# A decoder trunk with attention, gMLP and routed experts: side work of the gMLP dealt out anew over its steps, and weights loaded earlier

## What is computed

```python
for i in range(DEPTH):                       # DEPTH = 2
    h = x * (1 + sc_m) + sh_m
    y = sliding_window_sink_attention(h, ...) if i == 0 else chunked_spatial_gating(h, ...)
    x = layer_norm(DEEPNORM_ALPHA * x + (1 + gt_m) * y, ...)
    h = x * (1 + sc_f) + sh_f
    y = hierarchical_moe(h, ...)             # 4 groups of 8 experts, top 1 group, top 2 experts
    x = layer_norm(DEEPNORM_ALPHA * x + (1 + gt_f) * y, ...)

def chunked_spatial_gating(h, ...):          # the gMLP, chunks of 128 tokens
    u, v = split(gelu(h @ w_in + b_in))      # 2048 columns each
    v = layer_norm(v)
    mixed = einsum('gts,bnsgc->bntgc', tril(w_s), v) + b_s
    return (u * mixed) @ w_out + b_out
```

## Time and profile before

| | us |
|---|---|
| median of 3 runs | 2449.65 |
| the profiled execution: time, and its span | 2451.3, 2449.9 |
| TensorE busy, share of the span | 1326.5, 54% |
| VectorE | 1255.0, 51% |
| ScalarE | 639.9, 26% |
| GpSimd | 427.4, 17% |
| spans of the 8 cores | 2393.2 to 2449.9 |

### The profile page before, as it was taken

One profiled execution on the slowest core, in us unless ns is written; L12 is line 12 of the kernel. 1 busy time (PEld: TensorE's weight loads), 2 busy tenths in 40 slices (PEclk: granted clock), 3 DMA queues, 4 the chain that ended last, 5 costly groups with the idle time before them and its releaser, 6 DMA issues.

```text
span 2449.9 us, 30623 instructions; the slowest of 8 cores (2393.2 to 2449.9 us)
## 1 busy us (share of the span) xinstructions
PE 1326.5 (54%) x9631; PEld 810.8 (33%) x9631; DVE 1255.0 (51%) x2512; ACT 639.9 (26%) x1251; POOL 427.4 (17%) x558
## 2 busy tenths in 40 slices
PE   1537657766335464255227998989631744557300
PEld 0324434443223343134113443434311533335200
DVE  2344445545345354254218777777523534556388
ACT  1314424544311111012013444444211211112000
POOL 1000002010131111011101221313013211111242
PEclk9768878878667687678658999999965867778655
DMA  9979989985569998799982887879756899999762
GB/s 164 136 129 141 108 105 110 134 98 35 103 111 232 252 223 200 193 215 251 244 170 52 162 163 158 146 144 145 105 129 170 193 263 240 239 248 256 261 216 103
DMA packets 92621, 413.14 MB, mean 169 GB/s; under 512 B 21223, under 2 KB 21223, under 8 KB 80617
## 3 DMA queue, kind: packets, MB, share of 16 engines
q0 software_dynamic: 41344, 211.43, 58.7%
q1 hardware_dynamic: 51102, 199.60, 23.6%
HBM read 454.49 MB, written 165.25 MB: 253 GB/s over the span
## 4 chain that ended last, share of the span: by engine, by line
DMA 44%; PE 21%; DVE 17%; issue 9%; POOL 2%; ACT 2%; another core or an unknown queue 2%; SPq 1%; DVEq 1%; POOLq 0%; ACTq 0%
DMA sb_A<-adaP 7%; DMA sb_W<-wb 7%; DMA sb_x<-xd 6%; PE bank L1354 5%; DMA ys<-sb_hT 3%; DMA ys<-sb_Z 3%; PE bank L1672 2%; DMA sb_W<-ys,sb_idx 2%; DMA sb_A<-post_ln_b 2%; DMA sb_W<-attn_w_qkv 2%; DMA mod<-sb_adfm 2%; DMA sb_hT<-xd 2%; PE bank L1598 2%; DVE sb_hT L1379 2%; PE bank L1629 2%
## 5 line engine op out<-in xcount | busy, mean ns | idle before, releaser
L1354 PE MATMUL bank<-sb_hT,sb_W 128*128 128x256 bf16 x1984 | 308.4, 323 | 165.9 <-DMA sb_W<-wb 133.1
L1354 PEld LDWEIGHTS bank<-sb_hT,sb_W 128*128 128x128 bf16 x1984 | 223.4, 115 | 221.6 <-issue 168.9
L1336 ACT ACTIVATE sb_hT<-bank,sb_H 128x256 bf16<-128x256 f32 x256 | 130.4, 562 | 439.7 <-PE bank L1327 438.7
L1341 DVE TENSOR_SCALAR sb_hT<-bank,sb_H 128x256 bf16<-128x256 f32 x256 | 126.9, 537 | 194.8 <-PE bank L1327 160.1
L1379 DVE TENSOR_TENSOR sb_hT<-bank,sb_gtbf 128x512 f32<-128x512 f32 x176 | 121.5, 691 | 70.0 <-DMA ys<-sb_hT 52.4
L607 POOL TENSOR_TENSOR sb_rstdt<-sb_mvt,sb_eps_t 128x1 f32<-128x1 f32 x64 | 25.6, 401 | 684.6 <-DVE sb_R L445 275.6
L1375 PE MATMUL bank<-sb_W,sb_R 128*128 128x512 bf16 x496 | 132.8, 414 | 12.3 <-DVE sb_hT L1379 10.5
L1598 PE MATMUL bank<-sb_x,sb_Z 128*128 128x512 bf16 x512 | 130.0, 400 | 10.7 <-DVE sb_cact_rep L1653 7.4
L1672 PE MATMUL bank<-sb_W,sb_Z 128*128 128x512 bf16 x512 | 131.7, 404 | 2.2 <-ACT sb_Z L1665 2.2
L1629 PE MATMUL bank<-sb_x,sb_Z 128*128 128x512 bf16 x512 | 121.3, 379 | 0.7 <-issue 0.7
L1316 POOL DMA_INDIRECT sb_hT<-xh,sb_slots x64 | 61.0, 953 | 339.8 <-PE bank L1327 313.8
(11 more groups left out here) (248 smaller groups left out, 2700.5 us busy)
## 6 DMA issues: line engine op xcount, KB each, us to landing
wb<-moe_w POOLq DMA_DIRECT2D x41, 1536.0 KB, 20.6
sb_W<-wb SPq DMA_DIRECT2D x39, 1536.0 KB
ys<-sb_hT SPq DMA_DIRECT2D x44, 1024.0 KB
sb_W<-moe_w POOLq DMA_DIRECT2D x23, 1536.0 KB, 22.9
ys<-sb_Z SPq DMA_DIRECT2D x20, 1024.0 KB
sb_A<-adaP POOLq DMA_DIRECT2D x30, 512.0 KB, 16.3
sb_x<-xin SPq DMA_DIRECT2D x16, 512.0 KB, 11.1
xd<-sb_x SPq DMA_DIRECT2D x16, 512.0 KB, 36.3
```

Source lines behind the costliest of these rows:

```text
L1336: S.op("act", (lambda k=k, src=src: lambda e: e.activation(out=hTe[i][:, k, :], in_=src, func=AF.Identity, scale=H1[haff][:, k:k + 1], bia ...
L1341: S.op("dve", (lambda k=k, src=src: lambda e: e.tensor_scalar(out=hTe[i][:, k, :], in0=src, scalar1=H1[haff][:, k:k + 1], scalar2=H0[haff] ...
L1354: S.op("pe", (lambda k=k, f=f, fc=fc: lambda e: e.matmul(banks[bk][:, f * 256:(f + 1) * 256], wgu[:, k, fc:fc + 128], hTe[i][:, k, :], sta ...
```

## The change

The side work of a gMLP tile is put in other steps; its instructions are the same. New order, all for tile t's steps: cb 0: tl_combine(t+3). cb 1: ln_stats(t+3), the first half of affine(t+2), finalize_b(t-2). cb 2: ln_stats(t-1), the xd store of t-1, the gathers of t+4, ln_xhat(t+3), router_logits. cb 3: v_norm(t+1, 0), finalize_b(t+3), the second half of affine(t+2), ln_xhat(t-1), store_xh, the load of x[t+4], route_step. The loop has one step more at either end. Six blocks of w_in are loaded in the hooks of experts 20, 22, ... 30; blocks 6 and 7 and the output weights follow after the gathers of tile 0. `make_aset(2)` moves from step 59 to step 56.

```diff
-        def affine(t):
+        def affine(t, parts=(0, 1)):
...
-            if 28 <= e_ < 32:
-                win_load(e_ - 28)
+            if e_ >= 20 and e_ % 2 == 0 and e_ < 32:
+                win_load((e_ - 20) // 2)
...
-        def tl_fetch(u):
+        def tl_x(u):
             dma("sp", "dx", xv[u][0], xd_d[u * 128:(u + 1) * 128, :], reads=[Bxd[u]], writes=[xv[u][1]])
+
+        def tl_gather(u):
             for k in range(2):
...
-        for i in range(-13, 4 * NT + 15):
+        for i in range(-14, 4 * NT + 16):
             t, cb = divmod(i, 4)
-            if i == -12:
+            if i == -13:
+                win_load(6); win_load(7)
                 for c in range(4):
-                    win_load(4 + c)
                     wout_load(c)
...
                 gD(i - 3)
+            if cb == 0 and 0 <= t + 3 < NT:
+                tl_combine(t + 3)
+            if cb == 1 and 0 <= t + 3 < NT:
+                ln_stats(t + 3)
             if cb == 2 and 0 <= t - 1 < NT:
                 ln_stats(t - 1)
+                dma("sp", "dx", xd_d[(t - 1) * 128:t * 128, :], xv[t - 1][0], reads=[xv[t - 1][1]], writes=[Bxd[t - 1]])
+            if cb == 2 and 0 <= t + 4 < NT:
+                tl_gather(t + 4)
+            if cb == 2 and 0 <= t + 3 < NT:
+                ln_xhat(t + 3, xnb[0], Bxnb[0])
             if cb == 3 and 0 <= t + 1 < NT:
                 v_norm(t + 1, 0)
+            if cb == 3 and 0 <= t + 3 < NT:
+                finalize_b(t + 3, 0, 2, hdst=hTg[(t + 3) % 3], bhdst=BhTg[(t + 3) % 3], on_act=8)
+            if cb == 1 and 0 <= t + 2 < NT:
+                affine(t + 2, (0,))
+            if cb == 3 and 0 <= t + 2 < NT:
+                affine(t + 2, (1,))
             if cb == 3 and 0 <= t - 1 < NT:
                 ln_xhat(t - 1, xnb[1], Bxnb[1])
                 store_xh(t - 1, xnb[1], Bxnb[1])
-                dma("sp", "dx", xd_d[(t - 1) * 128:t * 128, :], xv[t - 1][0], reads=[xv[t - 1][1]], writes=[Bxd[t - 1]])
+            if cb == 3 and 0 <= t + 4 < NT:
+                tl_x(t + 4)
...
             if cb == 2 and t - 2 >= 0:
                 if t - 2 < NT:
                     router_logits(1, t - 2, hTr1, BhTr1)
+            if cb == 3 and t - 2 >= 0:
                 route_step(t - 2, 1)
-            if cb == 3 and 0 <= t + 3 < NT:
-                tl_combine(t + 3)
-                ln_stats(t + 3)
-            if cb == 3 and 0 <= t + 4 < NT:
-                tl_fetch(t + 4)
-            if 0 <= t + 2 < NT:
-                if cb == 0:
-                    ln_xhat(t + 2, xnb[0], Bxnb[0])
-                if cb == 1:
-                    finalize_b(t + 2, 0, 2, hdst=hTg[(t + 2) % 3], bhdst=BhTg[(t + 2) % 3], on_act=8)
-                if cb == 2:
-                    affine(t + 2)
-            if i == 4 * (NT - 1) - 1:
+            if i == 4 * (NT - 1) - 4:
                 make_aset(2, None, None, None)
```

More of the change, by code:

```diff
@@ L621, in ln_xhat @@
                  reads=[bxa, Brstd_[t], Bnmr], writes=[bdst])
-        def affine(t):
+        def affine(t, parts=(0, 1)):
             xa, bxa = xv[t]
[L625 to L630, removed]
+            if 0 in parts:
+                S.op("dve", lambda e: e.scalar_tensor_tensor(out=xa, in0=xa, scalar=mvt[:, t, 0:1], in1=A1[:],
+                                                             op0=ALU.subtract, op1=ALU.mult),
+                     reads=[bxa, Bmv_[t], BA1], writes=[bxa])
+            if 1 in parts:
+                S.op("dve", lambda e: e.scalar_tensor_tensor(out=xa, in0=xa, scalar=rstdt[:, t:t + 1], in1=A0[:],
+                                                             op0=ALU.mult, op1=ALU.add),
+                     reads=[bxa, Brstd_[t], BA0], writes=[bxa])
         def store_xh(t, src, bsrc):
```

## The result

The changed kernel takes 2516.4 us (median of 4 runs, 2510.95 to 2518.54), the kernel before in the same comparison 2448.2 us. The ratio is 1.0264, with a 95% interval of [1.0231, 1.0297]: **slower by 2.6%, 68 us**. The forecast was +42 us.

What follows compares the result with a forecast made beforehand. TensorE bounds the gMLP, with waits for transfers set by the weight conversions. Tiles +52 (394 against 342), `make_aset` -10, weight loads 0 gave +42 on the profiled 2451.3, stated as 2492 us; 8-in-10 range 2420 to 2545.

Steps and rivals of the forecast that it cites:

- The period is C + 12: gMLP tile: the period is 12 us plus C, the x load's landing counted from VectorE's end of the additions.
- The clear tile: gMLP tile whose x load meets no conversion: C 16.5, period 28.5 us; with a routing burst 33.
- The seven colliding tiles: Seven of eleven gated gMLP tiles: a conversion issued just before the x load makes C 25, period 37 us.
- The four tiles "taken as clear": Other gated gMLP tiles: an older conversion delays gathers, leaves the load a gap; two at 28.5, two at 33 us.
- The doubles: gMLP tiles 3 and 8, with two conversions each: about 12 us extra, counted half, adding 12 to the sum.
- The upper end: Worst end of the gMLP tiles' term: all eleven collide, 11 x 37 + 24 = 431, +89 us.
- `make_aset`: Near the gMLP's end: row loads issued earlier shorten VectorE's wait for post_ln_g; -10 us, ends 0 and -20.
- Weight loads: Two fewer behind tile 0's gather, -12 us; two more at the first MoE's end, +12; taken as 0.
- Gathers hidden by the load: gMLP combine: gathers land under the x load's cover, costing nothing extra; without that cover they would hold the combine.
- The likeliest case: Whole kernel: +42 us, 2492 us, own range 2470 to 2525; chance 0.50.
- Rival (c): Whole kernel: every tile collides, doubles whole, early weight loads delay the experts; +89 + 12 - 10, 2542 us; chance 0.12.
- Rival (a): gMLP x load slips ahead of conversions: -11 us in tiles; 2408 at best, 2430 with middle terms; chance 0.20.

Runs made afterwards that it cites:

- Run 3: Changed kernel with no conversions of layer 1's experts during the gMLP; 2517.3 us (one run), stores of tiles 0 to 11 312.6 us apart.
- run 2: Changed kernel with six x buffers instead of five (V's ring four, not six), x load still in cb 3; ratio 1.0194 to the kernel before.
- run 10: Kernel before with only `make_aset(2)` moved from step 59 to step 56; ratio 0.9967 to the kernel before.
- Runs 11 and 12: Kernel before with only the change's weight loads: ratio 0.9952; changed kernel with the old weight loads: ratio 1.0237, both to the kernel before.
- run 1: Changed kernel with six x buffers (V's ring four) and the x load right behind the previous tile's combine in cb 0; ratio 0.9885 to the kernel before.
- run 4: Changed kernel with each conversion split into two DMAs of half the columns; 2524.8 to 2572.7 us, 1.015 to the kernel before by two executions.
- run 6: Changed kernel with six x buffers (V's ring four) and the x load issued before xhat's store, in cb 3; ratio 0.9879 to the kernel before.

## Why the prediction was right, and where it was off

**The period is C + 12: right.** It is C + 11.6: 36.8 measured for C = 25.2, 50.7 for 39.2. Over the eleven tiles of core 3 the C's are 25.2, 33.5, 39.2, 24.0, 30.8, 24.1, 26.5, 35.9, 22.5, 31.0 and 25.4, in sum 318.1; with 11 x 12 that is 450, measured 445.2.

**The clear tile: shorter than foretold.** Run 3 has no conversion and took 27.2 us for a tile without a routing burst and 30.5 for one with it, where I had 28.5 and 33; in sum 312.6 against 331. The load went out at +11.3 and landed 3.7 later, where I had +10.8 and 5.7.

**The seven colliding tiles: right.** C = 25 was foretold; the single ones (t = 1, 4, 6, 9, 11) have 22.5 to 25.4.

**The four tiles "taken as clear": the step that failed.** C is 33.5, 30.8, 26.5 and 31.0, not 16.5 or the 21 that a period of 33 means. I wrote that an older conversion "delays the gathers and leaves the load a gap". On core 3 it delayed the xd store instead, to whose landing the load is tied by the buffer, and the load left at +17.0 to +17.6. In three of the four the next conversion stood beside it, issued at +6.7 to +7.0; in the fourth (t = 7) it came only at +24.3, and C is the lowest, 26.5. Expected for these four 2 x 28.5 + 2 x 33 = 123; measured 45.0 + 42.3 + 37.9 + 42.5 = 167.7: 45 us, most of the 51 by which this core's eleven tiles missed the 394. The tie to the store is the smaller part of it. In the mean of the cores the four take 157 us in the changed kernel and 151 in run 2, where the tie is gone and the load leaves at +11.2; run 3, without conversions, has 116. What I had wrong is the gap: in three of the four a young conversion stood beside the load too.

**The doubles count whole.** C 39.2 and 35.9, 14 and 11 above a single one. Together 25 us, of which I had counted 12: another 13 on core 3.

These two would make 394 + 45 + 13 = 452, against 445 on core 3; the cores' mean is 424. So the term was +52 where the cores' means moved by 69 and the slowest core's by 103. The upper end (431 us, +89) held the mean; cores 2 to 5 passed it, core 3 by 14 us. The 342 us that I started from were core 0's, the shortest of the eight; their mean was 354.6.

**`make_aset`: right.** -10 foretold; 8 us in the time of run 10, 9 in the wait. In the changed kernel the wait fell by 12.7 on the mean of the cores. The stretch of the four last tiles, three of which have no x load any more, got 20.4 shorter, `make_aset`'s part included; the rest of that I had not counted.

**Weight loads: 0, within the ends.** Runs 11 and 12 show both halves, 12 to 13 at the start and 16 to 29 on the other side, the latter unsure by some 10.

**Gathers hidden by the load: right**, as run 1 shows, which takes away the load: 21 us in nine waits.

**The sum.** +52 - 10 + 0 was forecast. On the cores' means, with the store's shift of one step (6.3 us) put back, it was +69.0 in the tiles, +12.7 before the first x load, -11.7 in the start, -15.3 in the last tiles and behind them, +2.4 in the rest: +57; the slowest core adds the remaining 9, since its tiles collided worst (66.5 from span to span). The likeliest case had the right mechanism and direction, and its own range 2470 to 2525 held the result. That the number came within 24 us is in part luck. From the slowest core before (0) to the slowest after (3) the tiles took 103 us more, not 52, and all the rest 36 less, not 10, most of it in the last tiles (-29.5): two misses of opposite sign. Rival (c), that everything collides, is what happened in the tiles; its other half came as well, +12.7 before the first x load, but was given back at the start, which (c) had excluded. Rival (a) needed a load that slips ahead of the conversion, and not one of eleven did. In 1356.4 to 1370.4, the load's time on the way, the queues of core 3 moved:

```profile
q0 software_dynamic: 52, 1.09, 50.7%
q1 hardware_dynamic: 288, 0.79, 14.2%
```

That is 52 packets of GpSimd's queue at 0.507 x 16 x 14 / 52 = 2.2 us each, and 288 of SyncE's at 0.11. That looks like the forecast's small packets that pay for large ones, but for the third of this time in which the engines moved nothing, and run 4, where five times smaller packets changed nothing. The prediction took the rows to agree with an alternation packet by packet; they showed only that load and conversion end together, and no run here shows the alternation.

## What to carry to other kernels

Moving a consumer earlier costs what its producer's slack was: count, from the event that frees the buffer, when the load may leave and when it is wanted, and take its landing beside the longest transfer of the stage, not alone (3.7 us and 13 here). A load with two holds that lie side by side (a buffer's store and a queue neighbour's wait) shows little or no gain when one is taken away; test both together before dropping either. And what stands in front of the first small transfers of a stage is on the path whole: six weight loads behind the gathers and not ahead of them were worth as much as half of what this change lost.

## What the runs showed of the hardware

Cutting the conversions' packets from 33 KB to 6 KB (3.7 to 0.6 us each) did not bring a load beside them down sooner: 14.2 us for 13.3. I had expected a price proportional to the packet, and have no experiment that says what it is proportional to instead.

The load of x takes 3.7 us without conversions and 13.3 with them, with the DMA engines idle for a third of the stage. In run 6 their share is 0.89, the load takes 18.9, and the combine waits a quarter as long, because the load leaves 11 us earlier. The DMA share of a stage does not say whether its small transfers are late; the time from their issue to their landing, beside the time at which they are wanted, does.
